# Modulation transposes inside a unit, sums of squares in three parts, rope tables later, a mixer's tail in pieces

## The reference, cut to what matters

```python
def rms_norm(x, g):
    y = xf * lax.rsqrt(jnp.mean(xf * xf, axis=-1, keepdims=True) + EPS)
    return (y * g.astype(jnp.float32)).astype(x.dtype)

def adaln(cond, prm):
    mod = jax.nn.silu(cond) @ prm["mod_w"] + prm["mod_b"]
    return jnp.split(mod, N_MOD, axis=-1)

def trunk_layer(xl, xc, c, c_ctx, prm, even, ctx_out, ropes):
    mod_l = adaln(c[:, None, :], prm)
    mod_c = adaln(c_ctx[None, None, :], prm)
    def half_ffn(x, m, name):
        sh, sc, g = m
        h = modulate(rms_norm(x, prm[name + "_norm"]), sh, sc)
        return x + 0.5 * g * swiglu(h, prm[name + "_w_in"], prm[name + "_w_out"])
...
def conv_module(u, prm):
...
    y = layer_norm(y, prm["conv_ln_g"], prm["conv_ln_b"])
    return jax.nn.silu(y)
```

## Time and profile before

| what | value |
|---|---|
| runs of the kernel | 3398.11, 3403.58, 3402.97 us, median 3402.97 |
| the profiled execution | 3398.24 us, its span 3396.5 us |
| TensorE busy | 3223.1 us, 95% |
| VectorE, ScalarE, GpSimd busy | 2026.9, 1428.2, 181.8 us |
| mean granted TensorE clock | 0.976 |
| DMA | 478.28 MB, mean 141 GB/s |

### The profile page before, as it was taken

One profiled execution on the slowest core, in us unless ns is written; L12 is line 12 of the kernel. 1 busy time (PEld: TensorE's weight loads), 2 busy tenths in 40 slices (PEclk: granted clock), 3 DMA queues, 4 the chain that ended last, 5 costly groups with the idle time before them and its releaser, 6 DMA issues. The chain is left out here.

```text
span 3396.5 us, 51226 instructions
## 1 busy us (share of the span) xinstructions
PE 3223.1 (95%) x20294; PEld 2865.6 (84%) x20294; DVE 2026.9 (60%) x2665; ACT 1428.2 (42%) x2342; POOL 181.8 (5%) x151
## 2 busy tenths in 40 slices
PE   5999999889999999999889999999999999999998
PEld 4878777468787788877579999899999999999998
DVE  4776759747777633335445566556466665654665
ACT  3333334633333322224454444445454544454543
POOL 1000011000000100020000000300000002100000
PEclk8999999989999999999999999999999999999999
DMA  7566632026666333332136656553556665543664
GB/s 226 156 180 180 172 95 78 13 69 177 176 188 183 101 87 108 88 101 87 50 86 170 178 165 181 157 173 100 148 160 187 177 185 153 166 132 109 177 180 130
DMA packets 769421, 478.28 MB, mean 141 GB/s; under 512 B 37973, under 2 KB 746165, under 8 KB 769093
## 3 DMA queue, kind: packets, MB, share of 16 engines
q1 hardware_dynamic: 767200, 474.88, 49.3%
q10 hardware_dynamic: 2020, 0.64, 0.1%
HBM read 474.40 MB, written 1.05 MB: 140 GB/s over the span
## 5 line engine op out<-in xcount | busy, mean ns | idle before, releaser
L537 PE MATMUL psum<-normed,weights_part 128*128 128x256 f32 (+1 forms) x7392 | 1311.0, 338 | 32.0 <-DVE normed L867 11.6
L537 PEld LDWEIGHTS psum<-normed,weights_part 128*128 128x128 f32 x7392 | 1140.7, 192 | 186.9 <-issue 35.7
L523 DVE TENSOR_TENSOR weights_part<-weights,weights_part 128x2048 fp32r<-128x2048 f32 (+1 forms) x413 | 884.9, 2143 | 365.1 <-ACT weights_part L515 364.8
L515 ACT ACTIVATE weights_part<-weights 128x2048 fp32r<-128x2048 f32 (+1 forms) x413 | 739.1, 1792 | 811.1 <-PE psum L537 418.7
L537 PE MATMUL psum<-hidden,weights_part 128*128 128x256 f32 (+1 forms) x4224 | 680.4, 323 | 0.0
L537 PEld LDWEIGHTS psum<-hidden,weights_part 128*128 128x128 f32 x4224 | 614.5, 191 | 61.2
L537 PE MATMUL psum<-unscaled,weights_part 128*128 128x256 f32 x4224 | 515.3, 285 | 8.9 <-DVE unscaled L675 6.8
L537 PEld LDWEIGHTS psum<-unscaled,weights_part 128*128 128x128 f32 x4224 | 511.2, 193 | 11.4 <-DVE unscaled L675 8.6
L1086 DVE SCALAR_TENSOR_TENSOR stage<-weights,cond,stage 128x768 f32<-128x768 f32 x294 | 281.0, 1018 | 0.0
L406 POOL TENSOR_TENSOR square<-square,rinvs 128x256 f32<-128x256 f32 (+1 forms) x39 | 57.2, 1467 | 2773.6 <-ACT rinvs L391 2772.1
L880 DVE TENSOR_TENSOR rinvs<-rinvs,psum 128x256 f32<-128x256 f32 (+1 forms) x88 | 45.8, 520 | 163.2 <-ACT rinvs L774 163.2
(11 more groups left out here) (445 smaller groups left out, 2650.6 us busy)
## 6 DMA issues: line engine op xcount, KB each, us to landing
weights<-in_l_ffn_w_in SPq DMA_DIRECT2D x176, 512.0 KB, 5.1
weights<-in_ffn_w_gu SPq DMA_DIRECT2D x176, 512.0 KB, 5.0
weights<-in_l_mod_w SPq DMA_DIRECT2D x168, 384.0 KB, 3.4
weights<-in_w_in SPq DMA_DIRECT2D x34, 1024.0 KB, 5.2
weights<-in_w_gate SPq DMA_DIRECT2D x64, 512.0 KB, 5.2
weights<-in_l_ffn_w_out SPq DMA_DIRECT2D x64, 384.0 KB, 4.1
weights<-in_ffn_w_down SPq DMA_DIRECT2D x64, 384.0 KB, 3.9
weights<-in_l_ffn_w_out SPq DMA_DIRECT2D x64, 320.0 KB, 3.3
```

Of the source, the lines that this page charges most:

```text
L515: k.nc.scalar.activation(k.parts[part][0][:, W], k.slots[slot][:, W], ACT.Copy).then_inc(k.high_done, 1)
L523: k.nc.vector.tensor_tensor(k.parts[part][1][:, W], k.slots[slot][:, W], k.parts[part][0][:, W].bitcast(F32), ALU.subtract).then_inc(k.spl ...
L537: mm = k.nc.tensor.matmul(to, left[a], right[b], start=first and n == 0, stop=last and n == len(PASSES) - 1)
```

## The change

1. `turn` of unit u is issued between the two tiles of an "in" unit (`(tile, kc) == (1, 0)`) and ahead of chunk 5 of 11 of an "out" unit, instead of behind the unit.
2. GpSimd adds one chunk fewer in every norm, and TensorE sums three parts (total of six chunks, seventh square, eighth square). In the halves at 512 tokens the first two parts stand ahead of the last three matmuls of the last unit. A wait for the last stream sum stands there too.
3. The rope angles and sines come behind unit 4 of `ffn2` of layer 1.
4. In the first mixer's tail the reciprocal is made in four pieces of 128 columns at steps 23 to 26, the scaling moves from steps 24 to 27 to 29 to 32, one unit's split is made in two halves (25, 26 on ScalarE, 27, 28 on VectorE) and the second unit's split moves behind the mixer; the four gates of the convolution come at steps 33 and 34.

```diff
-        for n in range(1, KD - 1):
+        for n in range(1, KD - 2):
...
+def sum_parts(k, pe, tokens, bank, some):
+    for n in some:
+        if n == 0:
+            pe.wait_ge(summed.sem, summed.base + KD - 3)
+        else:
+            pe.wait_ge(squared.sem, squared.base + KD - 2 + n)
+        part = (total, buffers[(KD - 2) % 2], buffers[(KD - 1) % 2])[n]
...
+    begun = 2 if tokens == TOK else 0
...
+                        if stream is not None and (tile, kc) == (1, 0):
+                            stream.turn(pe, at(spec, c))
                         mm = product_of_parts(k, k.psum[:, bank(spec, c) + tile, T], [pair_tiles(w)[:, tile, kc] for w in parts],
                                               [x[:, kc, T] for x in k.normed], kc == 0, kc == KD - 1)
                     mm.then_inc(k.unit_done, 1)
-                    if stream is not None:
-                        stream.turn(pe, at(spec, c))
...
+                        if stream is not None and kc == KH // 2:
+                            stream.turn(pe, at(spec, c))
+                        if s == len(specs) - 1 and c == KD - 1 and kc == KH - 1:
+                            if stream is not None:
+                                stream.wait_summed(pe)
+                            if begun:
+                                sum_parts(k, pe, tokens, sums_bank(k, first + total - 1), range(begun))
...
+                if s == 0 and between is not None:
+                    each_unit(dve, 0, BETWEEN, unit_in, looped(s))
+                    between.angles(dve)
...
-CONV_MEAN, CONV_VARIANCE, CONV_SCALED = 17, 22, 23
-HEAD_AHEAD = {28: 0, 31: 1}
+CONV_MEAN, CONV_VARIANCE, CONV_ROOT, CONV_SCALED = 17, 22, 23, 28
+OUT_HIGH, OUT_LOW = (25, 26), (27, 28)
...
-    k.ahead[out.name] = 2
+    k.ahead[out.name] = 1
...
-                    for c in ((0,), (1, 2), (3,), (), ())[s - N_HEAD_JOBS]:
+                    for c in ((), (0, 1), (2, 3), (), ())[s - N_HEAD_JOBS]:
...
-                if s == CONV_SCALED:
+                if CONV_ROOT <= s < CONV_ROOT + 4:
+                    piece = conv_inverse[:, (s - CONV_ROOT) * P:(s - CONV_ROOT + 1) * P]
                     dve.wait_ge(t["conv_root"].sem, t["conv_root"].base + 1)
-                    nc.vector.reciprocal(conv_inverse, conv_inverse).then_inc(t["conv_inverse"].sem, 1)
+                    nc.vector.reciprocal(piece, piece).then_inc(t["conv_inverse"].sem, 1)
```

More of the change, by code:

```diff
@@ L428, in _ @@
             following.begin(pe)
-        pe.wait_ge(summed.sem, chunks_summed)
         pe.wait_ge(k.banks_free, RING + last)
[L431 to L437, removed]
+        sum_parts(k, pe, tokens, sums_bank(k, last), range(begun, 3)).then_inc(t["added"].sem, 1)
         if following is not None:
@@ L696, in close, with half_ffn @@
         self.highs.close(KD), self.lows.close(KD)
-def half_ffn(k, tokens, name, layer, gain, shift, gate, stream=None, ahead=0, between=lambda engine: None, spread=None,
+def half_ffn(k, tokens, name, layer, gain, shift, gate, stream=None, ahead=0, between=None, spread=None,
              unscaled=None, following=None):
@@ L764, in _ @@
                 split(split_high, act, 0, q)
-            between(act)
+            if between is not None:
+                between.load(act)
             for s, spec in enumerate(specs):
@@ L794, in _ @@
                     prepare_sqrt(k)
-                each_unit(act, 0, spec.n, unit_in if s % 2 == 0 else unit_out, looped(s))
+                begun = 0
+                if s == 0 and between is not None:
+                    each_unit(act, 0, BETWEEN, unit_in, looped(s))
+                    between.tables(act)
+                    begun = BETWEEN
+                each_unit(act, begun, spec.n, unit_in if s % 2 == 0 else unit_out, looped(s))
         @block.tensor
@@ L871, in _ @@
                 split(split_low, dve, 0, q)
-            between(dve)
             for s, spec in enumerate(specs):
@@ L924, in unit_out @@
                         stream.accumulate(dve, at(spec, c))
-                each_unit(dve, 0, spec.n, unit_in if s % 2 == 0 else unit_out, looped(s))
+                begun = 0
+                if s == 0 and between is not None:
+                    each_unit(dve, 0, BETWEEN, unit_in, looped(s))
+                    between.angles(dve)
+                    begun = BETWEEN
+                each_unit(dve, begun, spec.n, unit_in if s % 2 == 0 else unit_out, looped(s))
             if stream is not None:
                 stream.derive(dve)
-        invert_rms(k, block, tokens, first + total - 1, spread, following)
+        invert_rms(k, block, tokens, first + total - 1, spread, following, begun)
     if following is not None:
@@ L1337, in even_mixer @@
     first, ready = spec.start, k.ahead[spec.name]
-    k.ahead[out.name] = 2
+    k.ahead[out.name] = 1
+    out_part, out_slot = k.parts[k.part_of[out.start]], k.slots[out.start % RING]
+    out_halves = [slice(n * WIDE // 2, (n + 1) * WIDE // 2) for n in range(2)]
     width, n_conv = HD + MLA_ROPE, 4
@@ L1811, in _ @@
                         place(h)
-                if s in HEAD_AHEAD:
-                    split_high(k, act, 0, out.start + HEAD_AHEAD[s])
+                if s in OUT_HIGH:
+                    half = out_halves[OUT_HIGH.index(s)]
+                    act.wait_ge(k.weights_ready[out.start % RING], out.ready[0])
+                    act.wait_ge(k.unit_done, k.part_before[out.start] + 1)
+                    last = nc.scalar.activation(out_part[0][:, half], out_slot[:, half], ACT.Copy)
+                    if s == OUT_HIGH[1]:
+                        last.then_inc(k.high_done, 1)
                 if CONV_MEAN < s <= CONV_MEAN + n_conv:
```

98 lines of the change are left out of this document (56 added, 42 removed).

## The result

The changed kernel takes 3503.15 us (median of 4 runs, 3501.08 to 3503.43), where the kernel before took 3403.27 beside it (4 runs, 3398.11 to 3403.89). The ratio is 1.0296, 95% interval 1.0278 to 1.0313: slower by 100 us. The forecast was 3483, and its range ended at 3502, 1.15 us short.

What follows compares the result with a forecast made beforehand. TensorE, busy 95% of the span, was taken as the bound. 72 + 20 + 4 - 10 - 2.8 = +83 on the profiled 3398.24 gave 3481, stated as 3483 us; range 3455 to 3502, the forecast's own 3472 to 3494.

Steps and rivals of the forecast that it cites:

- Waits of the transposes, +72: Mid-unit transposes in both streams: 94.4 us of new waits for VectorE's stage, the old 22.3 gone; +72 us.
- the formula: Transpose wait in "in" units: 0.6 + 1.9 m us, m the step's place in VectorE's body; "out" units computed separately.
- The clock, +20: Slow TensorE clock behind long transpose waits: seven per stream, 1.5 us each, less 1.3 already paid; +20 us, bounds 0 to 36.
- Sums of squares, +4: All norms, sums in three parts with two early at 512 tokens: +4 us, from 0 to +8.
- The -3.0 at the first mixer's output product: Norm after that product: the GpSimd add falls away, sums end near 743.4 instead of 746.4; -3.0 us.
- The first norm: The kernel's first norm: change to the sums of squares costs 1.0 us.
- the norm of 2155.95 and its twin: GpSimd's sixth chunk is itself late there, and a third part is added: 0, from -1 to +1 us each.
- Tail, -10: First mixer's tail: reciprocal in pieces and split in halves remove TensorE's long waits; -10 us, from -5 to -13.8.
- The leftover of the gates: Mixer's tail: two gates ahead of the last copy of probabilities, among the reasons some 4 of 13.8 us stay.
- Rope tables, -2.8: TensorE's 2.81 us wait behind the rope tables goes, covered by split weights at unit 5; -2.8 us, or 0.
- the second rival: Clock costs 36 us instead of 20, with a tail that gains only 5: 3504 us, chance 0.13.
- a poor tail: Within the dearer-clock case: the first mixer's tail gains only 5 us.

Runs made afterwards that it cites:

- the later place: Against the kernel with the mid-unit transposes alone: transposes asked at three quarters of a unit, ahead of chunk 8 in "out" units; 3451.04 us, ratio 1.0133.
- the earlier steps: Against the kernel with the mid-unit transposes alone: VectorE's modulation steps put ahead of its split of the next weights in "in" units; 3438.26 us, ratio 1.0100.
- The filled kernel: Against the kernel with the mid-unit transposes alone: useless extra products put ahead of 14 of the 21 transposes; 3489.84 us, ratio 1.0266.
- the sums behind: Against the kernel before: only the sums of squares in three parts, all three behind the last product; 3397.34 us, ratio 0.9983.
- the faster kernel of 3386 us: Against the changed kernel: transposes back behind their unit, all three sum parts behind the last product, tail and rope tables kept; 3386.36 us, ratio 0.9956.

## Why the prediction was wrong in size

**Bound and direction: right.** TensorE's queue sets the time, and the transposes in mid-unit cost far more than the rest of the change gains. The kernel with this part alone shows it (+107 of 100).

**Waits of the transposes, +72: 78.** Steps and order as predicted. The classes came 0.1 to 0.7 us above the formula (units 5 and 25: 3.0 to 3.2 for 2.5; units 2 and 22: 4.7 for 4.4; units 7, 19 and 27: 6.4 to 6.6 for 6.3), unit 34 has 4.53 for 3.4, units 10, 15 and 30 are exact to 0.15. That TensorE pays each in full is shown from both sides, by the later place and by the earlier steps. In every row the second tile's products, split and ready, stay behind the transposes. That agrees with the Trainium skill, "TensorE: Matmul & The Clock Gate", section "Step-by-step: what each phase is for", which states that matmuls keep program order.

**The clock, +20: 33. This is the step that failed.** It read "a wait of 3.4 us and more costs some 1.5 us beyond itself" and took "14 x 1.5 = 21". Both factors were low. Seventeen sets are slow and not 14: the waits of unit 34 and of unit 5 (3.17 and, in the second stream, 2.96) are among them. And a slow wait costs 33 / 17 = 1.9 us in this profile, not 1.5: 1.3 in the transposes and the rest in the products behind.

The price had been read at one place, where the products behind the transposes lost only 0.2 us (22.22 for 22.03). In the whole change they lose from 0.3 us to 1.6 (the 144 products at 134.22 took 34.30 us, and 32.95 in a stretch at full clock), and the longer wait is not always the dearer: behind 6.41 us they lost 0.3. The bound "3.4 us and more" was no bound either. Its own rows have transposes at 1.12 instead of 0.60 us behind waits of 3.06 and 2.64 us, and of the four waits of 3.41 to 3.42 us in the trace of before three had a full-speed set behind them (395.79, 859.94 and 1064.72); the forecast had read only the one at 189.58.

The filled kernel shows the mechanism. Its 1.0 to 1.4 us a wait is lower than 1.9, and why the price differs between places and kernels stays open. That the sets take 2.82 instead of 1.53 us while the granted clock falls agrees with the Trainium skill, "TensorE: Matmul & The Clock Gate", section "What's actually happening", which has an idle array run at 1.2 GHz, half of its full clock.

**Sums of squares, +4: +6.0 alone.** The mechanism at the halves holds (two parts in TensorE's busy time, the 1.7 us behind as empty as before), and they cost 7.1 us in the trace of this part alone, where 5.7 were forecast. What was left out is that work behind the empty time can run at the slow clock: the spread takes 2.08 us for 1.16 at the first half, and in the whole change, where the three cost 9 us, the eighth square's part 1.83 for 1.05. The -3.0 at the first mixer's output product did not come in full, -1.8 alone and -1.2 in the whole change, for the same reason: its two last parts took 1.87 and 1.85 us and not 0.95 and 1.05. The first norm cost 2.2 for 1.0, and the norm of 2155.95 and its twin gained 1.6 together, where 0 was forecast.

**Tail, -10: -9.2 alone,** and -12.6 in the trace of the whole change, which escaped a slow weighing (1.94 us where the tail alone has 2.95; its trace has -10.9). The leftover of the gates was named in the forecast.

**Rope tables, -2.8: -3.6 alone,** the wait gone and the cover at unit 5 sufficient, as predicted.

**The sum.** 78 + 33 + 6 - 9 - 4 = 104, with 99.9 measured, where the forecast had 80 over the median. The time is that of the second rival, a dearer clock at 3504, which had a chance of 0.13; the range stopped 2 us short of it, though the prediction says that it takes in most of that rival. That its number fits so well is luck. It was put together with a poor tail, which did not come, and with 36 for the clock, which came at 33; waits above the formula brought the rest. Two terms of one sign that hang on the same idle time should have stretched the range together.

## What to carry to other kernels

In front of an in-order engine, price a moved instruction as "ready minus asked", both measured from one event, and then add the slow clock for each wait of some 3 us and more; the sum of both is what the move costs. Work of TensorE that is independent of the last operand belongs behind the last product, in the time in which that operand is made, not ahead of it. And before an operation is put ahead in an engine's order, look for a wait inside it: whatever it jumps is held by that wait, which here turned 22 us of waits into 46 more at another place.

## What the runs showed of the hardware that was not expected

- One and the same wait can end at either clock. The four waits of 3.40 to 3.42 us of the transposes that stand behind their unit were looked at in seven kernels (the one before, the tail, the sums, the rope tables alone, the sums behind, the change but for the transposes, and the faster kernel of 3386 us): 13 of 28 had transposes of 1.8 us or more behind them, mostly 2.82, and the others 1.53 to 1.60. In mid-unit every wait of 3.85 us and more was slow (2.2 to 2.8 us), those of 2.96 to 3.69 us went either way, and two of 2.01 and 2.50 us were slow too.
- Useless products made the kernel faster: 270 extra matmuls of 512 columns in two streams, 14 to 19 us less (5 to 22 by the intervals), because TensorE did not idle ahead of the transposes.
